# Experts, crowded-expert path and per-layer input in one block; mixers' first low parts and biases reordered

## The reference, cut to what matters

```python
def _moe_ffn(x2d, ...):                 # top 4 of 32 experts for each token
    hg, hl = split(xblk @ w_gu[e] + b_gu[e])
    hg = minimum(hg, 7); hl = clip(hl, -7, 7)
    y = ((hl + 1) * hg * sigmoid(1.702 * hg)) @ w_down[e] + b_down[e]
    ...                                  # times the gate, added up by token
# first block, after the mixture (in words):
x  = DEEPNORM_ALPHA * x + mixture(x)
x  = x + sigmoid(x @ ple_gate_w) * (p @ ple_proj)
x  = layer_norm(x, ln2_g, ln2_b)
# second block
h = layer_norm(x, ln_in_g, ln_in_b)
for l in range(2):
    h = hybrid_layer(h, ...)             # input projection, HGRN, attention, memory; then layer_norm,
                                         # convolved gated feed-forward, layer_norm
```

## Time and profile before

| | us |
|---|---|
| median of 3 runs | 3742.3 (3741.82 to 3742.62) |
| the profiled execution | 3739.85 |
| its span | 3738.2 |
| PE busy | 3455.7 (92%) |
| DVE busy | 2528.2 (68%) |
| ACT busy | 1905.6 (51%) |
| POOL busy | 267.3 (7%) |

### The profile page before, as it was taken

The page is one execution under the profiler, slowest core; times in us unless marked ns, Lnnn a source line. Parts: engine busy times, 40 slices in busy tenths (PEclk is TensorE's granted clock), DMA queues, the critical chain, the costliest instruction groups (busy, mean ns, idle before and its releaser), DMA issues. The chain is left out here.

```text
span 3738.2 us, 44896 instructions
## 1 busy us (share of the span) xinstructions
PE 3455.7 (92%) x16696; PEld 2726.2 (73%) x16696; DVE 2528.2 (68%) x2847; ACT 1905.6 (51%) x2130; POOL 267.3 (7%) x234
## 2 busy tenths in 40 slices
PE   9998778999999999998789987999998898799998
PEld 7875256787878777787558775678887786578886
DVE  6644548999999999997367766366527667646642
ACT  4212226777777777776265345244316435524422
POOL 0000001111111112111010000010001000010000
PEclk9988788999999999999889999999999999899999
DMA  4110028999999999996221120223312112023231
GB/s 148 40 29 23 0 89 340 362 360 361 360 355 365 359 360 349 361 360 252 85 71 57 57 84 18 61 94 101 102 62 85 57 40 88 18 71 107 97 102 62
DMA packets 116209, 597.10 MB, mean 160 GB/s; under 512 B 20434, under 2 KB 21858, under 8 KB 65794
## 3 DMA queue, kind: packets, MB, share of 16 engines
q1 hardware_dynamic: 102754, 577.78, 42.9%
q0 software_dynamic: 13312, 17.35, 1.9%
HBM read 585.01 MB, written 26.80 MB: 164 GB/s over the span
## 5 line engine op out<-in xcount | busy, mean ns | idle before, releaser
L2164 DVE TENSOR_TENSOR wl<-raw,wh 128x2048 fp32r<-128x2048 f32 x384 | 876.2, 2289 | 67.5 <-ACT wh L2099 65.1
L2099 ACT ACTIVATE wh<-raw 128x2048 fp32r<-128x2048 f32 x384 | 735.3, 1915 | 214.0 <-PE pu L2046 161.9
L2044 PE MATMUL pu<-wh,Xh 128*128 128x512 f32 x1024 | 413.8, 404 | 0.0
L2046 PE MATMUL pu<-wh,Xl 128*128 128x512 f32 x1024 | 407.4, 398 | 0.0
L2045 PE MATMUL pu<-wl,Xh 128*128 128x512 f32 x1024 | 404.9, 395 | 0.0
L3857 ACT ACTIVATE w_high<-w_raw 128x1024 fp32r<-128x1024 f32 (+1 forms) x120 | 137.1, 1145 | 333.4 <-PE acc L3831 172.0
L3888 DVE TENSOR_TENSOR w_low<-w_raw,w_high 128x1024 fp32r<-128x1024 f32 (+1 forms) x120 | 159.6, 1331 | 195.7 <-PE ps L3789 104.4
L3813 PE MATMUL ps<-x_high,w_high 128*128 128x512 f32 x656 | 255.4, 389 | 0.0
L3814 PE MATMUL ps<-x_low,w_high 128*128 128x512 f32 x656 | 255.3, 389 | 0.0
L2044 PEld LDWEIGHTS pu<-wh,Xh 128*128 128x128 f32 x1024 | 193.2, 189 | 49.8 <-issue 8.0
L2046 PEld LDWEIGHTS pu<-wh,Xl 128*128 128x128 f32 x1024 | 192.9, 188 | 46.3
(11 more groups left out here) (698 smaller groups left out, 6900.0 us busy)
## 6 DMA issues: line engine op xcount, KB each, us to landing
raw<-in_exp_w SPq DMA_DIRECT2D x384, 1024.0 KB, 7.7
w_raw<-in_w_in SPq DMA_DIRECT2D x100, 512.0 KB, 3.4
w_raw<-in_w_up SPq DMA_DIRECT2D x88, 512.0 KB, 3.8
w_raw<-in_w_down SPq DMA_DIRECT2D x32, 704.0 KB, 4.0
w_raw<-in_w_out SPq DMA_DIRECT2D x32, 384.0 KB, 3.1
w_raw<-in_w_mem_kv SPq DMA_DIRECT2D x16, 512.0 KB, 4.2
w_raw<-in_w_out SPq DMA_DIRECT2D x8, 512.0 KB, 3.9
w_raw<-in_ple_gate_w SPq DMA_DIRECT2D x8, 512.0 KB, 3.9
```

The lines of the kernel that those rows point to most:

```text
L2044: nc.tensor.matmul(o, lh[:, k, :], wh[:, m % PARTS, c], start=(m >= 8 and kh == 0 and kk == 0), stop=False)
L2046: mm = nc.tensor.matmul(o, ll[:, k, :], wh[:, m % PARTS, c], start=False, stop=end)
L2099: nc.scalar.activation(wh[:, m % PARTS, :], raw[:, m % RAW, :], ACT.Copy).then_inc(w_high, 1)
L2164: nc.vector.tensor_tensor(wl[:, m % PARTS, :], raw[:, m % RAW, :], wh[:, m % PARTS, :], ALU.subtract).then_inc(w_low, 1)
```

## The change

The three stages `experts`, `rest_of_experts` and `embedding` become one stage, in `mixture`. The crowded-expert path and the per-layer input become classes whose parts are called from the queues of the block, and their buffers lie over those of the experts that are free by then.

```diff
@@ SP, after the experts' loads
                 all_experts(sp, expert)
                 sp.wait_ge(spilled, 16)
+                sp.wait_ge(w_low, (EXPERTS - 1) * CHUNKS + 7)
+                ple.sync_proj(sp)                      # 8 DMAs, ple_proj
+                sp.wait_ge(w_low, (EXPERTS - 1) * CHUNKS + 8)
+                ple.sync_p(sp)                         # 1 DMA, p
+                rest.sync(sp, used)
+                sp.wait_ge(used, (EXPERTS - 1) * CHUNKS + 8)
+                for n in range(3):
+                    ple.sync_gate(sp, n)
+                sp.wait_ge(scattered, EXPERTS * 16)
+                ple.sync_y(sp)                         # 4 DMAs, y_rows
+                for n in range(3, DT):
+                    ple.sync_gate(sp, n)
@@ PE
                 all_experts(pe, expert)
+                rest.tensor(pe, y_ready)
+                ple.tensor(pe)
@@ ACT
                 turned_high(EXPERTS - 1, 1)
+                ple.scalar_p(act)                      # split p
+                act.wait_ge(w_low, (EXPERTS - 1) * CHUNKS + 10)
+                ple.scalar_proj(act)                   # split ple_proj
                 for d in (0, 1):
                     weighted(EXPERTS - 1, 1, d)
+                rest.scalar(act)
+                ple.scalar(act)
@@ DVE
                 turned_low(EXPERTS - 1, 1)
+                ple.vector_p(dve)
+                ple.vector_proj(dve)
+                rest.vector(dve, used)
+                dve.wait_ge(used, EXPERTS * CHUNKS)
+                ple.vector(dve)
@@ RestOfExperts (every engine that takes part)
+    def some(self, eng):
+        eng.wait_ge(self.over_ready, 1)
+        return eng.If(eng.value_load(self.over[0:1, 0:1]) > 0)
@@ Embedding.scalar: the first two gate tiles are split while e is taken, not while x is split
         for t in range(DT):
             act.wait_ge(self.e_made, t + 1)
             nc.scalar.activation(self.e[:, t, :], acc[t % 2], ACT.Copy)...
+            if t in (2, 5):
+                high_part(t // 3)
         for k in range(DT):
             act.wait_ge(self.added, k + 1)
             nc.scalar.activation(self.high[:, k, :], self.x[:, k, :], ACT.Copy)...
-            if k == 0: high_part(0)
-            if k == 3: high_part(1)
@@ Embedding.vector: low_part(0) and low_part(1) moved from behind the splits of x to before them
@@ class Norm
-    def pool_biases(self, pool):
-        for j in range(DT):
-            pool.wait_ge(self.low_ready, j + 1)
-            nc.gpsimd.tensor_scalar(self.x[:, j, :], self.x[:, j, :], self.bias(j), None, ALU.add)...
+    def act_bias(self, act, j):
+        act.wait_ge(self.low_ready, j + 1)
+        self.K.nc.scalar.activation(self.x[:, j, :], self.x[:, j, :], ACT.Identity, bias=self.bias(j))...
@@ mixers, ACT
                     for n in range(0, 4):
                         after(n)
-                        if n == 2 and layer == 0:
-                            act.wait_ge(turned, 1)
-                            (the two Sin activations)
+                        norm.act_bias(act, 2 * n)
+                        norm.act_bias(act, 2 * n + 1)
+                    if layer == 0:
+                        act.wait_ge(turned, 1)
+                        (the two Sin activations)
@@ mixers, DVE (rope_tables cut into rope_angle 2, rope_turns 3, rope_rest 3 and rope_quarter 2 operations, layer 0 only)
                     low_part(1)
-                    rope_tables()
+                    rope_angle()
                     low_part(2)
                     (lb, 1 small operation)
+                    rope_turns()
                     low_part(3)
+                    rope_rest()
                     low_part(4)
+                    rope_quarter()
                     low_part(5)
                     clamp(0)
                     (neglam, 2 small operations)
+                    low_part(6)
                     accumulate(0)
-                    low_part(6)
                     near(0)
@@ feed_forward: POOL's queue is gone
                     middle(n, 1)
+                    if n < DT:
+                        norm.act_bias(act, n)
                     act.wait_ge(sides, n * 4 + 4)
```

More of the change, by code:

```diff
@@ L1875, with mixture @@
 ROWS = S + SLOTS
-def experts(K, x, gates, kept, b_in, over, spill, w, bias, x_rows, y_rows):
+def mixture(K, a, x, gates, kept, gain, shift):
     nc = K.nc
+    w, spill, x_rows, y_rows = a["exp_w"], a["expert_rows"], a["x_rows"], a["y_rows"]
+    b_in, bias = a["exp_b_down"], a["bias_parts"]
     with ExitStack() as ctx:
[L1882 to L1888, removed]
-        few = K.sb(ctx, "few", [EXPERTS, 2])
[L1890 to L1896, removed]
+        over = K.sb(ctx, "over", [1, 2], I32)
+        few = K.sb(ctx, "few", [EXPERTS, 2])
         trash = K.sb(ctx, "trash", [P, 2])
@@ L1901, in experts @@
         gneg = K.sb(ctx, "gneg", [P, 2])
-        rl = K.sb(ctx, "rl", [P, 512])
-        sg = K.sb(ctx, "sg", [P, 512])
+        top = K.sb(ctx, "top7", [P, 2])
+        pos = K.sb(ctx, "pos", [P, NT, EXPERTS])
+        gpart = K.sb(ctx, "gpart", [P, NT, EXPERTS, 4], F32R)
+        routed = K.sb(ctx, "routed", [P, NT, EXPERTS])
+        before = K.sb(ctx, "before", [P, NT - 1, EXPERTS])
+        b_down = K.sb(ctx, "b_down", [P, 2 * P])
         vc = K.sb(ctx, "vc", [P, 512])
[L1905 to L1908, removed]
         y = K.sb(ctx, "y", [P, 2, D])
+        with ExitStack() as held:
+            rows = K.sb(held, "rows", [P, D])
+            Xh = K.sb(held, "Xh", [P, DT, SLOTS], F32R)
+            Xl = K.sb(held, "Xl", [P, DT, SLOTS], F32R)
+            sel = K.sb(held, "sel", [P, NT, SLOTS], F32R)
+            brow = K.sb(held, "brow", [P, 512], F32R)
+            ones = K.sb(held, "ones2", [P, P], F32R)
+            rl = K.sb(held, "rl", [P, 512])
+            sg = K.sb(held, "sg", [P, 512])
+            hb = K.sb(held, "hb", [P, 2, 512])
+            hh = K.sb(held, "hh", [P, FE // P, SLOTS], F32R)
+            hl = K.sb(held, "hl", [P, FE // P, SLOTS], F32R)
+            wh = K.sb(held, "wh", [P, PARTS, CW], F32R)
+            wl = K.sb(held, "wl", [P, PARTS, CW], F32R)
+            raw = K.sb(held, "raw", [P, RAW, CW])
         pu = K.ps(ctx, "pu", [P, 4, 512])
@@ L1912, in experts @@
         pt = K.ps(ctx, "pt", [P, 512])
[L1913 removed]
+        pslot = K.mu
         px = pu
@@ L2539, in tiles, with first_block @@
 def tiles(x, n=DT):
     return [x[:, t, :] for t in range(n)]
-def mixture(K, a, x, gates, kept):
-    with ExitStack() as ctx:
-        over = K.sb(ctx, "over", [1, 2], I32)
-        experts(K, x, gates, kept, a["exp_b_down"], over, a["expert_rows"], a["exp_w"], a["bias_parts"], a["x_rows"], a["y_rows"])
-        rest_of_experts(K, over, a["mixture_in"], a["exp_w"], a["exp_b_gu"], a["expert_rows"], x)
-def first_block(K, a, x):
+def first_block(K, a, x, outer):
     nc = K.nc
```

525 lines of the change are left out of this document (270 added, 255 removed).

## The result

The changed kernel takes 3683.2 us (median of 4 executions, 3679.5 to 3688.3) against 3742.5 (4 executions, 3741.8 to 3745.2): ratio 0.984, 95% interval 0.983 to 0.986. That is 59.2 us gained, where 40.2 were predicted. The profiled execution of after took 3688.3 (span 3686.5), 5 above its median; between the two profiles the gain is 51.7.

A forecast was written before the change was run, and what follows sets the result against it. PE, busy 92% of the span, was taken as the bound, with gains only where it waits. Terms 29.1 + 0.6 - 0.7 + 6.2 + 5.0 = 40.2 took 3739.85 to 3699.7; plus 2.45 to the median, 3702.1, range 3695 to 3712.

The forecast's parts named there:

- so nothing can be won there: Experts: PE busy 997.8 of 1000 us at full clock, so no gain was counted; what is left lies where PE waits.
- The embedding, 29.0 forecast: Per-layer input after the experts: earlier loads and splits let PE turn y_tokens at 1781.7 instead of 1810.8, gain 29.1 (27 to 31.5).
- The 0.6 of the gate tile: Gate tile 0 in the embedding: its low part is made earlier, gain 0.6, between -1.6 and 1.
- the 0.7 of the barriers: End of `lasting`, now behind the per-layer input, and a larger clear: -0.7, between -0.4 and -1.1.
- Mixers 0, 6.2 (3.5 to 7.5): Layer 0 mixers: tile 2 ends 6.2 earlier, then ACT binds; tile 7 ends 6.7 earlier, less half a clock fall.
- The wait for `take(4)`: Layer 0 mixers: `take(4)` ends at 1940.7 and releases tile 6, for which PE waits 1.6.
- Mixers 1, 5.0 (3 to 6): Layer 1 mixers: tile 6 goes on without its 3.11 wait and tile 7 ends earlier, gain 5.1, taken as 5.0.
- Biases 0, barriers and branch: Biases off POOL cost 0 on the path; barriers -0.7; crowded-path branch costs 0 below running matmuls, or 0.5 + 3.5.
- Rival A: Biases bind ACT in both mixers, 5.3 us a layer; layer 0 gains 1.4, layer 1 nothing: 3711.9; chance 0.14.
- C: ACT's table switches ahead of `take(4)` cost the Trainium skill page's price, 4.1 more: 3706.2; chance 0.04.
- D: Slower: PE's jump in the experts' loop fetches like the crowded-path jump, 50 against 40 gained: 3752; chance 0.03.
- B: Loads early, branch ahead, turning at 1779.1, barrier at its bound, no clock falls in mixers: 3696.9; chance 0.12.

The follow-up runs named there:

- before_weights_moved: Kernel before, with 96 bytes put ahead of rows and 64 ahead of hh, so the experts' weights match their moving side modulo 256: 3721.8 us against 3740.6, ratio 0.995.
- after_off32: Kernel after, with 32 bytes put ahead of wh and of y_tokens, so wh, wl and raw lie 32 bytes past a multiple of 64: 3701.1 us.
- before_mixers: Kernel before with only the mixers' and feed-forwards' part of the change: 3732.0 us, ratio 0.997.
- after_aligned: Kernel after, with 128 bytes ahead of cs and of the arrival's y_high, moving both matmul sides in mixers and feed-forwards: 3681.5 us.
- after_low6_late: Kernel after, with only the low part of tile 6 put behind the sums again: 3688.9 us.
- after_pool_biases: Kernel after, with the mixers' biases on POOL again and the feed-forwards' left on ACT: 3681.5 us.
- the bench: Separate measurements, not the model: groups of 240 matmuls issued like the experts', with moving side and weights at varied byte offsets; 226.7 to 237.3 ns a matmul.
- the third sweep: The benches' pass beside ACT's and DVE's copies, against two with other engines idle; in the first bench the three agree within 0.1 ns.

## Why the prediction was wrong

**The failed step** stands in its first paragraph: PE is busy for 997.8 of 1000 us at full clock, "so nothing can be won there". From a busy share it concluded that the length of a matmul is fixed. In the kernel before the experts' groups had 395 to 397 ns where the feed-forward's matmuls of the same shape had 389: that difference was to be seen in its profile, and the diff moves raw, wh and wl to other places. Both were passed over, and the experts stood in the sum at nothing. The missing term is the experts' 18.8 us (before_weights_moved; 18.0 by after_off32), 4.1 ns for each of 4608 matmuls.

The traces divide it. PE's advance fell by 5.4 ns a matmul, 22.6 us over the 4216 steps that could be compared (23.4 in before_weights_moved). Against that stand PE's waits for gathered rows, which vary from one profile to the next: 4.6 us before, 6.6 in after, 2.2 to 11.4 in the ten kernels with matched places. Without these waits the experts took 1162.9 to 1165.5 us in those ten, and 1183.6 to 1186.1 in before, before_mixers and after_off32, where the places are unequal by 32 bytes or more than 64. So the places are worth about 21 us of PE's time, and the waits decide how much of it an execution shows.

With 18.8 the sum is 40.2 + 18.8 = 59.0, against 59.2 measured. That it comes so close is luck in part, since the other terms err in both directions: 28.2 instead of 29.0, about 4.6 instead of 6.2, and 6.7 instead of 5.0.

**The embedding, 29.0 forecast** (29.1 + 0.6 - 0.7): 28.2 between the profiles, 28.2 to 31.0 in the other kernels that have this part as after has it. Right, and by its mechanism: PE's turning waits for the y loads. These were issued 5.8 behind the scatter's issue (6.2 forecast), e began at once and took 11.0 (10.9 to 12.8 forecast). The 0.6 of the gate tile and the 0.7 of the barriers were not measured by themselves.

**Mixers 0, 6.2 (3.5 to 7.5).** Between the two profiles it is 0.5, which looked like a miss. before_mixers shows 6.7, and the tile that the prediction followed bears it out: PE ended tile 7 at 56.2 behind the stage's first matmul in the kernel before, at 49.7 in before_mixers and at 51.1 in after, where 6.7 earlier was forecast. The wait for `take(4)` was forecast at 1.6 and is 1.53 in after. What after lost again is the clock: over the profiles of nine kernels with the new order and the biases on ACT the layer took 524.2 to 530.6, mean 528.0, with 53 to 70 us at half clock, and over four with the old 531.1 to 534.1, mean 532.6. So about 4.6, inside the range.

**Mixers 1, 5.0 (3 to 6).** 6.6 to 6.8 in the pairs that differ in this part; the kernels with the new order had 520.8 to 521.8, but for after_aligned with 524.0 and 60 us at half clock. The mechanism was right: after_low6_late alone brings all of it back. At tile 7 the gain is 4.9 (52.0 to 47.1 behind the stage's first matmul), against 5.1 forecast. The mis-sized term is the clock behind it: the time at half clock fell by 13.7 us (66.8 to 53.1), of which 10.4 lie in the stage's first 150 us and the rest later, where I had reckoned with one stretch behind one wait.

**Biases 0, barriers and branch.** The feed-forwards differ by 0.1, and the branch costs nothing. Rival A is refuted by before_mixers' 6.7 in each layer and by after_pool_biases, whose trace puts the biases' price on ACT at 1.2 us in layer 0, not 5.3. C is refuted by ACT's rows in after: its table loads ahead of `take(4)` take 1.28 each, with no more than 0.02 between one and the activation ahead of it or behind it. D is refuted by the loop, whose branch takes 76 to 254 ns on PE in after as it did before. B was right in that the branch runs ahead of PE.

## What to carry to other kernels

Before a stretch is called bound by PE, compare the mean of one matmul with that of the same shape in other stages: 395 against 389 ns is 3% of the 227 ns by which PE advances. A stretch in which PE is busy for 99.8% can still get shorter. In loops of matmuls that each load their own weights, let the weights' and the moving side's arrays begin at the same place modulo 256 bytes, and treat any change in the order of allocation as a change in speed: 32 bytes were worth 18 us here, in two different stages. When comparing two profiles, hold a layer's half-clock time next to its length before a gain is called lost.

## What was not expected of the hardware

- A matmul of 128x128 weights and 512 moving columns of fp32r, each with its own weight load, advances by 226.7 to 226.9 ns if weights and moving side begin equal modulo 256 bytes (0, 32, 128 and 160 tried), and by 228.9 to 234.3 if not; 4 bytes of difference cost most, 237.3. The experts and the feed-forward agree in sign, with 5.4 ns and 5.9 to 6.1 ns a matmul. That PE's weight load and its moving reads run side by side and get into each other's way is the obvious reading; it was argued, not shown, and the bench's 64 against 320 bytes (228.9, 233.3) says that the rule is not complete.
- Neither the transfers' target nor ACT's and DVE's traffic beside PE changed that: 32 bytes under raw cost nothing, and the third sweep of each bench, beside the first 421 us of which ACT and DVE ran, is as the first two.
- The same order of work took 524 to 531 us in mixers 0, with 53 to 70 us at half clock, from one kernel's profile to the next. A layer's gain below 5 us was not to be read from one pair of profiles.
